# MLP up-projections with the weights stationary, both parts of the input side by side, and relu tiles kept feature-major

## The reference

```
def sq_relu_mlp(h, w_in, w_out):          # h: 256 x 1024
    return jnp.square(jax.nn.relu(h @ w_in)) @ w_out
```

## Time and profile before

| | us |
|---|---|
| median of the timed runs | 1688.16 |
| span of the profiled execution | 1689.1 |
| TensorE matmul busy | 1569.3 |
| VectorE busy | 919.9 |
| ScalarE busy | 675.9 |
| GpSimd busy | 168.8 |

### The profile page before, as it was taken

The page is one execution under the profiler, slowest core; times in us unless marked ns, Lnnn a source line. Parts: engine busy times, 40 slices in busy tenths (PEclk is TensorE's granted clock), DMA queues, the critical chain, the costliest instruction groups (busy, mean ns, idle before and its releaser), DMA issues.

```text
span 1689.1 us, 20919 instructions
## 1 busy us (share of the span) xinstructions
PE 1569.3 (93%) x8496; PEld 1344.0 (80%) x8496; DVE 919.9 (54%) x1048; ACT 675.9 (40%) x850; POOL 168.8 (10%) x144
## 2 busy tenths in 40 slices
PE   5998898888999989999999899998999989889998
PEld 5787897887888888678888898776888888768886
DVE  5678667564444455754444574355444447554444
ACT  5551000014443454555444434444444453554443
POOL 0012202110211300001111100000111100001110
PEclk9998998898999989999999999999999999989999
DMA  8310000005555533214555555434555544135551
GB/s 279 125 63 25 1 1 1 1 7 193 176 185 186 196 132 140 101 60 164 175 190 182 193 177 197 149 125 141 183 183 189 181 155 169 64 136 185 188 178 71
DMA packets 34919, 230.17 MB, mean 136 GB/s; under 512 B 4208, under 2 KB 4912, under 8 KB 8224
## 3 DMA queue, kind: packets, MB, share of 16 engines
q1 hardware_dynamic: 33040, 223.59, 38.6%
q0 software_dynamic: 1808, 5.56, 1.0%
HBM read 228.07 MB, written 1.05 MB: 136 GB/s over the span
## 4 chain that ended last, share of the span: by engine, by line
issue 65%; PE 22%; DVE 7%; POOL 3%; ACT 2%; POOLq 0%; DMA 0%; SPq 0%; DVEq 0%; ACTq 0%
POOL arena L1267 3%; PE bank L1658 3%; PE bank L1379 3%; PE bank L1380 3%; PE bank L1381 3%; PE bank L1654 3%; PE bank L1637 2%; DVE arena L1058 1%; DVE wlo L750 1%; DVE arena L1060 1%; PE bank L1486 1%; DVE arena L917 1%; ACT whi L398 1%; DVE arena L1127 0%; DVE arena L1145 0%
## 5 line engine op out<-in xcount | busy, mean ns | idle before, releaser
L1379 PE MATMUL bank<-whi,XH 128*128 128x512 f32 x1408 | 555.7, 395 | 11.2 <-DVE XL L779 9.4
L1380 PE MATMUL bank<-wlo,XH 128*128 128x512 f32 x1408 | 550.4, 391 | 0.0
L1381 PE MATMUL bank<-whi,XL 128*128 128x512 f32 x1408 | 550.2, 391 | 0.0
L815 DVE TENSOR_TENSOR wlo<-raw,whi 128x2048 fp32r<-128x2048 f32 x112 | 256.7, 2292 | 282.0 <-ACT whi L487 269.4
L750 DVE TENSOR_TENSOR wlo<-raw,whi 128x2048 fp32r<-128x2048 f32 x96 | 222.3, 2318 | 202.8 <-ACT whi L398 189.9
L1379 PEld LDWEIGHTS bank<-whi,XH 128*128 128x128 f32 x1408 | 266.1, 189 | 69.1 <-issue 8.9
L487 ACT ACTIVATE whi<-raw 128x2048 fp32r<-128x2048 f32 x112 | 214.7, 1917 | 240.5 <-PE bank L1381 240.5
L1381 PEld LDWEIGHTS bank<-whi,XL 128*128 128x128 f32 x1408 | 265.6, 189 | 55.9
L1380 PEld LDWEIGHTS bank<-wlo,XH 128*128 128x128 f32 x1408 | 265.9, 189 | 53.7
L398 ACT ACTIVATE whi<-raw 128x2048 fp32r<-128x2048 f32 x96 | 183.7, 1913 | 211.7 <-PE bank L1381 211.7
L1267 POOL TENSOR_TENSOR arena<-arena 128x512 f32<-128x512 f32 x64 | 110.7, 1748 | 1028.3 <-ACT arena L471 1028.3
(11 more groups left out here) (234 smaller groups left out, 1469.0 us busy)
## 6 DMA issues: line engine op xcount, KB each, us to landing
raw<-in_w_mlp SPq DMA_DIRECT2D x128, 1024.0 KB, 4.8
raw<-in_w_rv SPq DMA_DIRECT2D x8, 1024.0 KB, 4.8
raw<-in_w_rg SPq DMA_DIRECT2D x8, 1024.0 KB, 4.8
raw<-in_w_reo SPq DMA_DIRECT2D x8, 1024.0 KB, 4.9
raw<-in_w_k SPq DMA_DIRECT2D x4, 1024.0 KB, 11.6
raw<-in_w_v SPq DMA_DIRECT2D x4, 1024.0 KB, 5.4
raw<-in_w_r SPq DMA_DIRECT2D x4, 1024.0 KB, 4.7
raw<-in_w_rwo SPq DMA_DIRECT2D x4, 1024.0 KB, 4.8
```

The costliest lines, as they stand in the source:

```text
L815: dve.tensor_tensor(wlo[:, slot % SPLIT_RING], raw[:, slot], whi[:, slot % SPLIT_RING].bitcast(F32), ALU.subtract).then_inc(lo_done, 1)
L1379: pe.matmul(out_, xh[xs], wh[ws], start=start, stop=False)
L1380: pe.matmul(out_, xh[xs], wl[ws], start=False, stop=False)
L1381: return pe.matmul(out_, xl[xs], wh[ws], start=False, stop=stop_)
```

## The change

XH and XL become the two halves of one tensor XHL, so that the high and low part of an input tile lie side by side. In an up unit a 128 x 128 tile of weights is stationary. The high weights meet 512 moving columns (high input, low input) in one matmul, the low weights meet the 256 columns of the high input in a second one that adds to the first half of the bank. An up unit is 4 feature tiles x 4 k tiles x 2 = 32 matmuls. The result is feature-major: columns 0 to 255 of a bank hold high x high + low x high, columns 256 to 511 high x low. A tile t of 128 features and 256 tokens then goes through six small operations: ScalarE copies the second half out of PSUM (`low_half`), VectorE adds the first half (`full_sum`), GpSimd takes relu (a tensor_scalar with max) and squares, ScalarE takes the high part from SBUF (`hidden_hi`), VectorE the low part from SBUF (`hidden_lo`). There are no transposes of hidden tiles. UPL, UPZ and HID have two slots each, and the hidden tiles in XH and XL eight. The loops on all five engines are written out, with constant waits. The down units are as before.

```diff
+        XHL = sb("XHL", [P, 2 * KT, 2, T], F32R)
+        XH, XL = XHL[:, :, 0], XHL[:, :, 1]
+        UPL, UPZ, HID = at(8240, 2, T), at(8752, 2, T), at(9264, 2, T)
...
 # ScalarE
+                def low_half(t):
+                    if t % 4 < 3:
+                        act.wait_ge(up_done, (t0 + t) // 4 * 3 + t % 4 + 1)
+                    else:
+                        act.wait_ge(unit_used, b + (t - 3 if t > 3 else 2))
+                    if t0 + t >= 2:
+                        act.wait_ge(up_sum, t0 + t - 1)
+                    act.activation(UPL[:, t % 2], psum[up_bank(t)][:, T:2 * T], ACT.Copy).then_inc(up_low, 1)
+                def hidden_hi(t):
+                    act.wait_ge(square_done, t0 + t + 1)
+                    act.activation(XH[:, KT + t % 8], HID[:, t % 2], ACT.Copy).then_inc(h_hi, 1)
+                for j in range(MLP_STEPS):
+                    ua = b + (4 * j - 2 if j else 0)
+                    hi_upto(ua + 3)
+                    low_half(4 * j)
+                    low_half(4 * j + 1)
+                    low_half(4 * j + 2)
+                    hi_upto(ua + 4)
+                    low_half(4 * j + 3)
+                    hidden_hi(4 * j)
+                    hidden_hi(4 * j + 1)
+                    hidden_hi(4 * j + 2)
+                    hidden_hi(4 * j + 3)
+                    if j:
+                        hi_upto(ua + 6)
...
 # VectorE
+                def full_sum(t):
+                    dve.wait_ge(up_low, t0 + t + 1)
+                    if t0 + t >= 2:
+                        dve.wait_ge(square_done, t0 + t - 1)
+                    dve.tensor_tensor(UPZ[:, t % 2], psum[up_bank(t)][:, 0:T], UPL[:, t % 2], ALU.add)\
+                        .then_inc(up_sum, 1)
+                def hidden_lo(t):
+                    dve.wait_ge(h_hi, t0 + t + 1)
+                    dve.tensor_tensor(XL[:, KT + t % 8], HID[:, t % 2], XH[:, KT + t % 8].bitcast(F32), ALU.subtract)\
+                        .then_inc(h_lo, 1)
+                for j in range(MLP_STEPS):
+                    ua = b + (4 * j - 2 if j else 0)
+                    lo_upto(ua + 3)
+                    full_sum(4 * j)
+                    full_sum(4 * j + 1)
+                    full_sum(4 * j + 2)
+                    lo_upto(ua + 4)
+                    full_sum(4 * j + 3)
+                    for f in range(UK):
+                        hidden_lo(4 * j + f)
+                    if j:
+                        lo_upto(ua + 6)
...
 # GpSimd
+                for t in range(4 * MLP_STEPS * i, 4 * MLP_STEPS * (i + 1)):
+                    pool.wait_ge(up_sum, t + 1)
+                    if t >= 2:
+                        pool.wait_ge(h_lo, t - 1)
+                    pool.tensor_scalar(HID[:, t % 2], UPZ[:, t % 2], 0.0, 1.0, ALU.max, ALU.mult).then_inc(relu_done, 1)
+                    pool.wait_ge(relu_done, t + 1)
+                    pool.tensor_tensor(HID[:, t % 2], HID[:, t % 2], HID[:, t % 2], ALU.mult).then_inc(square_done, 1)
...
 # TensorE
+                def up(u, j, kg):
+                    pe.wait_ge(lo_done, u + 1)
+                    for f in range(UK):
+                        t = 4 * j + f
+                        bank = psum[up_bank(t)]
+                        if kg == 0 and t >= 4:
+                            pe.wait_ge(up_sum, t0 + t - 3)
+                        for k in range(UK):
+                            kt = kg * UK + k
+                            if t == 0 and kt % 2 == 0:
+                                pe.wait_ge(turned_lo, SPLIT0[TI[name]] + kt // 2 + 1)
+                            ws = (slice(None), u % SPLIT_RING, k, slice(f * P, (f + 1) * P))
+                            pe.matmul(bank[:, :], whi[ws], XHL[:, kt].rearrange("p h t -> p (h t)"),
+                                      start=(kt == 0), stop=False)
+                            ins = pe.matmul(bank[:, 0:T], wlo[ws], XH[:, kt], start=False, stop=(kt == KT - 1))
+                        if kg and f < UK - 1:
+                            ins.then_inc(up_done, 1)
+                    ins.then_inc(unit_used, 1)
+                for j in range(MLP_STEPS):
+                    ua = b + (4 * j - 2 if j else 0)
+                    up(ua, j, 0)
+                    up(ua + 1, j, 1)
+                    if j:
+                        down(ua + 2, 0, j - 1)
+                        down(ua + 3, 1, j - 1)
```

More of the change, by code:

```diff
@@ L173, in build @@
         wlo = sb("wlo", [P, SPLIT_RING, UK, UN], F32R)
-        XH = sb("XH", [P, 2 * KT, T], F32R)
-        XL = sb("XL", [P, 2 * KT, T], F32R)
+        XHL = sb("XHL", [P, 2 * KT, 2, T], F32R)
+        XH, XL = XHL[:, :, 0], XHL[:, :, 1]
         vecs = sb("vecs", [P, len(VECS), KT])
@@ L216, in build, with up_bank @@
         XN, JUNK = at(4096, MT, D), at(6144, 2, UN)
-        RELU = at(8240, MT, UN)
+        UPL, UPZ, HID = at(8240, 2, T), at(8752, 2, T), at(9264, 2, T)
+        def up_bank(t):
+            return (0, 1, 2, 3)[t] if t < 4 else (0, 1, 6, 7)[t % 4]
         hT, xxT = at(0, KT, T), at(2048, KT, T)
@@ L294, in build @@
             "pss_done", "pms_done", "psd_done", "ptmp_done"))
-        relu_done, square_done, h_turned, h_hi, h_lo = (sem(n) for n in (
-            "relu_done", "square_done", "h_turned", "h_hi", "h_lo"))
+        up_done, up_low, up_sum, relu_done, square_done, h_hi, h_lo = (sem(n) for n in (
+            "up_done", "up_low", "up_sum", "relu_done", "square_done", "h_hi", "h_lo"))
         dve_step, pool_step = sem("dve_step"), sem("pool_step")
@@ L368, in _ @@
                     continue
[L369 to L380, removed]
+                for i in range(MLP_UNITS):
+                    load_unit(name, U0[name] + i, i)
             for i in range(4):
@@ L465, in mlp @@
             def mlp(i):
[L466 to L492, removed]
@@ L493, in mlp @@
-                done[0] = b + MLP_UNITS - 1
-                hidden_hi(s0 + MLP_STEPS - 1, KT + 4)
+                b, t0 = U0[f"mlp{i}"], 4 * MLP_STEPS * i
+                def low_half(t):
[6 more added lines that the diff above has]
+                    act.activation(UPL[:, t % 2], psum[up_bank(t)][:, T:2 * T], ACT.Copy).then_inc(up_low, 1)
@@ new lines, in hidden_hi @@
+                def hidden_hi(t):
+                    act.wait_ge(square_done, t0 + t + 1)
+                    act.activation(XH[:, KT + t % 8], HID[:, t % 2], ACT.Copy).then_inc(h_hi, 1)
+                hi_upto(b + 2)
+                for j in range(MLP_STEPS):
[12 more added lines that the diff above has]
+                        hi_upto(ua + 6)
@@ L798, in mlp @@
             def mlp(i, plain):
[L800 to L808, removed]
-                lo_upto(b + 2)
[L811 to L821, removed]
+                b, t0 = U0[f"mlp{i}"], 4 * MLP_STEPS * i
+                def full_sum(t):
[8 more added lines that the diff above has]
+                        .then_inc(h_lo, 1)
+                lo_upto(b + 2)
+                for j in range(MLP_STEPS):
[10 more added lines that the diff above has]
+                        lo_upto(ua + 6)
                 lo_upto(b + MLP_UNITS)
@@ L1328, in _ @@
             pool.dma_start(SPREAD.rearrange("p k f -> p (k f)"), a["head_spread"]).then_inc(spread_in, 16)
-            pool.wait_ge(h_lo, 2 * MLP_STEPS)
+            pool.wait_ge(h_lo, 4 * MLP_STEPS)
             pool.memset(fKP, 0.0).then_inc(zeroed, 1)
@@ L1418, in mlp @@
             def mlp(i):
[L1419 to L1431, removed]
-                    ins.then_inc(unit_used, 1)
@@ L1434, in hidden_turn @@
[L1434 to L1442, removed]
@@ L1444, in down @@
-                def down(u, n, first, last, k0=KT):
+                b, name, t0 = U0[f"mlp{i}"], f"mlp{i}", 4 * MLP_STEPS * i
+                def up(u, j, kg):
[15 more added lines that the diff above has]
+                            ins.then_inc(up_done, 1)
+                    ins.then_inc(unit_used, 1)
@@ L1445, in down @@
+                def down(u, n, j):
+                    pe.wait_ge(lo_done, u + 1)
+                    if n == 0:
+                        pe.wait_ge(h_lo, t0 + 4 * (j + 1))
                     for k in range(UK):
@@ L1447, in down @@
                             ins = passes(psum[2 + 2 * n + m][:, :], (XH, XL), (whi, wlo),
-                                         (slice(None), k0 + k, slice(m * P, (m + 1) * P)), (slice(None), u, k),
-                                         first and k == 0, last and k == UK - 1)
+                                         (slice(None), KT + 4 * (j % 2) + k, slice(m * P, (m + 1) * P)),
+                                         (slice(None), u % SPLIT_RING, k), j == 0 and k == 0,
+                                         j == MLP_STEPS - 1 and k == UK - 1)
                     ins.then_inc(unit_used, 1)
[L1453 to L1477, removed]
+                for j in range(MLP_STEPS):
[5 more added lines that the diff above has]
+                        down(ua + 3, 1, j - 1)
                 for n in range(2):
```

(3 more changed lines are left out.)

## The result

The changed kernel takes 1802.67 us (1801.98 to 1806.93) against 1688.03: ratio 1.068, 95% interval 1.067 to 1.069. The forecast was 1728, range 1704 to 1762: the sign was right, the loss of 114.6 us is almost three times the 40 us forecast. The profiled execution has a span of 1801.5 us, 112.4 above the 1689.1 of the kernel before.

What follows compares the result with a forecast made beforehand. TensorE, busy 93% of the span, was taken as the bound; each step gains 0.69 us and waits 2.05. 32 x (2.05 - 0.69) = 43.5, less 3.5, gives +40.0 us: 1728, range 1704 to 1762, its high end from a 3.05 us wait.

Steps and rivals of the forecast that it cites:

- 28.8 and 3.5 us: TensorE: savings from removing 256 transposes (28.8 us) and four waits for the squares of a last pass (3.5 us together).
- the loops and the layout: Written-out loops were costed at nothing, with ends of minus and plus 0.1 us a pass.
- the order on ScalarE: ScalarE issues all four high copies before the next split but one, so TensorE waits once a step, 32 times in all.
- Rival A: The hidden chain stays hidden and TensorE's saving comes through whole: 1662.6 us; chance 0.11.
- Rival C: Weight loads do not hide where matmul widths alternate, adding 72 us: 1800 us; chance 0.03.
- Its relu of 256 columns is 0.47: GpSimd's relu in the hidden chain, set at 0.47 us for each of two tiles.
- the estimated 0.52: GpSimd's square of 256 columns, 0.52 us, estimated from the slope between squares of 512 and 2048 columns.
- the low parts were to hold GpSimd for 0.7 us a step: VectorE's low parts, with two SBUF inputs, block GpSimd's reads: 0.3 us at the start and 0.4 us later.
- the forecast's 8.05: End of GpSimd's last square, 8.05 us after TensorE ends a step's second up unit: 5.2 + 0.3 + 2.1 + 0.4.
- 1.95 us of wait: TensorE's wait once a step: down units end at 10.88, the next unit's split is ready at 12.85 us.
- rival B: TensorE's clock halves for 3.4 us after each wait, adding 1.7 us a step, 54 us: 1782 us; chance 0.09.
- 0.347: Up unit on TensorE: a pair of 512- and 256-column matmuls costs 0.347 us, a unit 5.55 in place of 5.44.

Runs made afterwards that it cites:

- e1_order: Changed kernel with the split of one next unit, on ScalarE and VectorE, moved ahead of the last two hidden tiles; 1676.37 us, 0.993 of before.
- e4_unrolled_before: Kernel before, with its loops written out and XH and XL as halves of XHL, all else as before; 1689.22 us, 1.000 of before.
- e10_vector_square: Changed kernel with relu and square as one VectorE operation after each sum, four slots for hidden tiles, no GpSimd in the MLPs; 1670.84 us, 0.989 of before.
- e2_filler: Changed kernel with eight unneeded transposes of the identity on TensorE after the two down units of each step; 1800.2 us.
- e6_max_only: Changed kernel with the relu as a tensor_scalar of one operation (max with 0), without the multiplication by 1; 1758.02 us.
- e3_ring4: Changed kernel with four slots in place of two for the sums and for the hidden tiles; 1751.81 us.
- e7_mult_form: Changed kernel with the relu's max replaced by a multiplication by 1, which leaves the relu out; 1710.98 us.
- e11_vector_square_nowait: e10_vector_square without TensorE's waits for the sums of tiles 2 and 3 of each MLP; 1666.90 us, 0.986 of before.

## Why the prediction was wrong

Right, by its own steps: the transposes and their waits went, and e1_order's time fits the 28.8 and 3.5 us set for them; the loops and the layout cost nothing (e4_unrolled_before); the order on ScalarE puts the split behind the last high copy, and TensorE waits once a step (e1_order takes it away). Rival A would have come from a shorter chain, and nearly did in e10_vector_square. Rival C fell: a pair has a pitch of 0.354 us, no load shows.

Wrong: the step "Its relu of 256 columns is 0.47". The row was a tensor_scalar of the right shape with another operation. It measured 1.07, twice in the chain, and the square 0.61 for the estimated 0.52. Another term was wrong the other way and hid part of this: the low parts were to hold GpSimd for 0.7 us a step, and in the changed kernel they held it for 0.03. In the pass above the last square ends at 9.26: the forecast's 8.05, with 0.5 for a later start of the third relu (most of it VectorE's split beside a square), 1.2 for the two relus, 0.2 for the two squares, less 0.7 for the collisions. The sum was made with 1.95 us of wait; the trace has 2.8 to 3.1 in most steps. The waits are 72.1 + 20.8 + 4.3 us, less the 4.6 of the five waits for line 750 before: 92.6 for the 32 x 1.95 = 62.4 forecast, +30 us. The 4.3 of these are waits for sums, which the forecast did not have. From the longer wait the second miss follows: rival B was priced nearly right (1.7 us a fall, 1.6 measured) but held as another outcome with a chance of 0.09, while it comes on top of the wait, behind 21 of 28. +34 us. The third term is small: the pair at 0.354 for 0.347, 64 x (5.66 - 5.55) = +7 us. 30 + 34 + 7 = 71 of the 72.4 us between the forecast span of 1729.1 and 1801.5. The high end of the range failed the same way: it allowed a wait of 3.05 us and no clock loss with it.

The rule taken from the Trainium skill, "TensorE: Matmul & The Clock Gate", Part 1, that the lower clock comes back after an idle window, made me think a wait of 2 us harmless. The runs decide otherwise: waits of 1.83 us and 2.20 us were followed by 0.70 and 0.65, though not each wait of that length was. What decides it stays open: behind waits that were mostly 1.8 to 2.2 us long the clock fell in 20 of 28 cases in e2_filler, in 11 in e6_max_only and in 10 in e3_ring4, so the length alone does not. In e3_ring4 the first stretch behind the wait of 1.83 us was this:

```profile
500.40:503.80 3.40, 3.40 (x15) 2.93 (x16) 2.29 (x1) 0.10 (x1) 0.00 (x0) 0.70 0.75 236
```

## What to carry to other kernels

Before you price a chain, look for a row with the same operation on the same engine, not only the same shape; where none exists, the range must hold more than twice the nearest row: here it was 1.07 for 0.47. An instruction that waits for a long chain must not stand in a queue ahead of work that the bounding engine needs soon; move either the work or the chain, the two were worth 126 us (e1_order) and 132 us (e10_vector_square) here. And a repeated wait of TensorE can have two prices, the idle time and the clock behind it: add them, they are not rivals.

## What the runs showed of the hardware

- Repeated TensorE waits, the mean clock, and behind how many of 28 waits it fell: up to 1.4 us (e7_mult_form) 0.969, none; 1.8 us in most steps (e3_ring4) 0.963, 10; 2.0 us in most steps (e6_max_only) 0.960, 11; 2.8 to 3.1 us in most steps 0.949, 21. Eight short transposes ahead of a wait of 2.0 to 2.2 us did not hold it (0.951, 20); 22, with waits of 0.4 to 0.95 us, did (0.969, none). A fall cost about 1.6 us.
- GpSimd's tensor_scalar on 128x256 float32: 0.40 us for mult and mult, 0.85 for max, 1.07 for max and mult. VectorE does max and the multiplication that squares in one operation of 0.42 to 0.43 us (e11_vector_square_nowait).
- VectorE with two SBUF inputs and GpSimd held each other both ways: a relu of 1.07 us took 3.11 across a split, a split of 2.29 took 2.69 and a low part of 0.42 took 0.86 behind a square. Not every overlap did: in the changed kernel all 32 low parts that began 0.5 us into a relu took 0.42 to 0.43 us, so there the later one was not blocked. Spans on GpSimd are rough, and why is open.
